# Routing, last scatter and last rows of a one-layer decoder step: logits turned, a short root, other banks and pieces

## The reference, cut to what matters

```python
mix, ... = token_mixers(rmsnorm(h, norm_mix_g), ...)
h = h + mix                                        # output projection w_out, 1024 x 1024
m = rmsnorm(h, norm_moe_g)
logits = m @ w_router + b_router                   # 1024 x 32
top_v, top_i = lax.top_k(logits, 4); gates = softmax(top_v)
h = h + sum over the four experts of gates * (act(m @ w_up[e] + b_up[e]) @ w_down[e] + b_down[e])
gate = sigmoid(rmsnorm(h, norm_ple_g) @ w_ple_gate)   # 1024 x 1024
h = h + (p @ w_ple_proj) * gate
y = rmsnorm(h, norm_final_g)
```

## Time and profile before

| | us |
|---|---|
| median of three runs (lowest, highest) | 1142.45 (1142.18, 1144.15) |
| the profiled execution's own time | 1142.76 |
| its span (first to last instruction or transfer in the trace) | 1141.0 |
| PE busy | 1088.5 (95%) |
| DVE busy | 379.8 (33%) |
| ACT busy | 156.2 (14%) |
| mean transfer rate over the span | 380 GB/s |

### The profile page before, as it was taken

The page is one execution under the profiler, slowest core; times in us unless marked ns, Lnnn a source line. Parts: engine busy times, 40 slices in busy tenths (PEclk is TensorE's granted clock), DMA queues, the critical chain, the costliest instruction groups (busy, mean ns, idle before and its releaser), DMA issues.

```text
span 1141.0 us, 16346 instructions
## 1 busy us (share of the span) xinstructions
PE 1088.5 (95%) x6463; PEld 443.6 (39%) x6463; DVE 379.8 (33%) x966; ACT 156.2 (14%) x351; POOL 32.3 (3%) x79
## 2 busy tenths in 40 slices
PE   9999999999999999999998899999999898989896
PEld 6663454333333333333333243333333333333332
DVE  3866565232222323222221223131313131313155
ACT  3543122100000000000001010000000000000022
POOL 2300120000000000000000000000000000000000
PEclk9999999999999999999999899999999999999998
DMA  8923967999999999999999999999999999999941
GB/s 300 308 111 123 380 238 294 427 427 426 428 426 427 428 428 428 428 429 428 427 430 427 428 428 426 428 427 430 427 430 428 428 429 428 428 429 427 421 156 42
DMA packets 41748, 433.86 MB, mean 380 GB/s; under 512 B 6105, under 2 KB 7265, under 8 KB 17134
## 3 DMA queue, kind: packets, MB, share of 16 engines
q1 hardware_dynamic: 40224, 428.74, 89.9%
q0 software_dynamic: 1424, 4.47, 1.2%
q10 hardware_dynamic: 62, 0.14, 0.0%
HBM read 429.03 MB, written 4.30 MB: 380 GB/s over the span
## 4 chain that ended last, share of the span: by engine, by line
PE 68%; DMA 26%; DVE 3%; ACT 1%; issue 1%; DVEq 0%; SPq 0%; ACTq 0%
PE bank L1042 28%; DMA ring<-in_w_up_dram 26%; PE bank L1088 12%; PE bank L1026 6%; PE bank L626 6%; PE bank L748 3%; PE bank L1010 3%; PE bank L650 1%; PE bank L1072 1%; PE bank L608 1%; DVE arena L1544 1%; PE bank L1117 1%; PE bank L934 1%; PE bank L1007 1%; PE bank L1078 1%; PE bank L858 1%
## 5 line engine op out<-in xcount | busy, mean ns | idle before, releaser
L1042 PE MATMUL bank<-ring,aT 128*64 128x512 f32 x1536 | 348.6, 600 | 27.6 <-DMA ring<-in_w_up_dram 27.3
L1042 PEld LDWEIGHTS bank<-ring,aT 128*64 128x64 f32 x1536 | 106.8, 137 | 253.7 <-issue 200.4
L1088 PE MATMUL bank<-ring,arena 128*64 128x512 f32 x768 | 169.6, 594 | 0.2
L1957 DVE TENSOR_TENSOR h<-h,bank 128x512 f32<-128x512 f32 (+1 forms) x96 | 65.6, 684 | 179.5 <-PE bank L1026 177.2
L1042 PE MATMUL bank<-arena,aT 128*64 128x512 f32 x512 | 115.7, 596 | 3.5 <-DMA arena<-in_w_up_dram 3.5
L1974 DVE TENSOR_SCALAR arena<-bank 128x256 f32<-128x256 f32 x64 | 27.2, 424 | 236.1 <-PE bank L1042 234.8
L1983 DVE COPY aT<-bank 64x512 f32<-64x512 f32 x32 | 22.2, 694 | 245.0 <-PE bank L1088 245.0
L1386 ACT ACTIVATE arena<-arena 128x256 f32<-128x256 f32 x64 | 26.7, 417 | 549.3 <-DVE arena L1974 549.3
L1088 PEld LDWEIGHTS bank<-ring,arena 128*64 128x64 f32 x768 | 53.8, 137 | 100.9 <-issue 98.2
L1026 PE MATMUL bank<-aT,arena 128*128 128x512 f32 (+1 forms) x192 | 83.5, 622 | 1.4 <-DVE aT L1983 0.9
L1042 PEld LDWEIGHTS bank<-arena,aT 128*64 128x64 f32 x512 | 35.2, 136 | 77.7 <-issue 69.8
(11 more groups left out here) (341 smaller groups left out, 740.5 us busy)
## 6 DMA issues: line engine op xcount, KB each, us to landing
ring<-in_w_up_dram SPq DMA_DIRECT2D x96, 2048.0 KB, 32.6
ring<-in_w_down_dram SPq DMA_DIRECT2D x48, 2048.0 KB, 33.2
arena<-in_w_up_dram SPq DMA_DIRECT2D x32, 2048.0 KB, 33.0
arena<-in_w_down_dram SPq DMA_DIRECT2D x16, 2048.0 KB, 33.3
ring<-in_w_in_dram SPq DMA_DIRECT2D x3, 2048.0 KB, 13.3
ring<-in_w_in_dram SPq DMA_DIRECT2D x4, 1024.0 KB, 11.9
ring<-in_w_out_dram SPq DMA_DIRECT2D x1, 4096.0 KB, 13.8
ring<-in_w_ple_gate_dram SPq DMA_DIRECT2D x2, 2048.0 KB, 13.5
```

The source lines that it names most:

```text
L1042: mm = pe.matmul(bank[n][CAP * hf:CAP * hf + CAP, :], xT[:, odd, 2 * j + a, :], up_cols(x, j, a, hf, n), start=False, stop=(j == 3 and a = ...
L1088: mm = pe.matmul(bank[4][CAP * hf:CAP * hf + CAP, :], actT[:, b, t, :], tile_of(x, UP_TILES + t)[:, 1024 * b + 512 * hf:1024 * b + 512 * h ...
L1957: tt(part, part, bank[5 + j % 2][at:at + ROWS[c], :], ALU.add).then_inc(s_free[j % 2], 1)
```

## The change: what it does

1. **Logits.** `turned_logits(c)` makes the router weights stationary (128 x 32) and lets the tokens move; slice k goes to rows 32(k mod 4) of a bank, so that four partial sums stand one below another. ACT copies them out (`logits_out`), and one product with `sel32` (four unit matrices of 32, one below the other) adds them up and turns them back. `sel32` is made by DVE just before `mix_done`.
2. **Root of chunk 1** (in routing, and again at the very end). ACT takes the square root; DVE takes the reciprocal and does one Newton round. A `Sqrt` without use stands ahead of it on ACT.
3. **Order in routing.** PE gathers most of chunk 0 between other work, DVE makes the selection columns right after the counts, ACT copies one turned half of chunk 1 that DVE copied before, two groups of `keep_clock` products are gone (2 and 3 products), one stays, and the last stays.
4. **Last scatter.** Each of the five products has a bank of its own (5, 6, 0, 1, 3) and waits for no addition. `moe_done` is gone; the last stage waits for each chunk by `h_ok`.
5. **Last gate product.** The second half of chunk 1 is computed as two pieces of 256 columns. ACT takes the gate halves of chunk 0 as they come. For chunk 1 DVE multiplies by the gain before the root is known; then ACT scales one half and writes it out by its own queue, DVE the other.

```diff
+            def turned_logits(c, ks=range(KD)):
...
+                    at = T_S * (k % 4)
+                    mm = pe.matmul(o[at:at + NE, 0:ROWS[c]], wrt[:, k, :], aT[:, k, TOK[c]], start=(k < 4), stop=(k >= 4))
...
+            def logits(c):
+                stored(pe, ("lgT", c))
+                o = open_bank(("lg", c))
+                close_bank(("lg", c), pe.matmul(o[0:ROWS[c], 0:NE], lgs[:, TOK[c]], sel32, start=True, stop=True))
...
+            turned_logits(2)
+            out_product(1, 0, range(4, 6))
+            pe.wait_ge(S["mix_done"], 1)
             logits(2)
-            out_product(1, 0)
+            out_product(1, 0, range(6, 8))
             turn_rows(0)
             out_product(1, 1, range(4, 6))
+            turned_logits(0)
+            turn_rows(1, (0,))
             logits(0)
-            turn_rows(1, (0,))
             out_product(1, 1, range(6, 8))
...
-            keep_clock(2, 5, parts_0)
-            logits(1)
...
+            chunk_0(range(3))
+            turned_logits(1, range(0, 4))
+            turned_logits(1, range(4, 8))
             pe.wait_ge(S["m3_ok"], 1)
-            pe.wait_ge(S["sel0_ok"], 1)
+            pe.wait_ge(S["sel0_ok"], 4)
             for d in range(KD):
                 cols, out = pass_columns(d)
...
+                pe.matmul(out, mbs[0:96, cols], sel[0:96, 0, 2, :], start=False, stop=False)
+            logits(1)
+            chunk_0(range(3, 7))
...
+            for j, ((c, hf), b) in enumerate(zip(SCATTER, LAST_BANK)):
...
+            for n, c in enumerate(ORDER):
+                pe.wait_ge(S["h_ok"], 2 * n + 2)
                 transposed(("nT", c, 0), h, c)
                 transposed(("nT", c, 1), h, c, 4)
...
             half_squares(0)
+            logits_out(0)
+            o = filled(act, ("mT", 1, 0))
+            act.activation(aT[:, 0:4, TOK[1]], o[:, :].rearrange("p (k t) -> p k t", k=4), ACT.Copy).then_inc(freed(("mT", 1, 0)), 1)
+            act.activation(rs_m[:, 0:1], ss_x[:, 1:2], ACT.Sqrt)
             half_squares(1)
+            act.wait_ge(S["hss"], 4)
+            act.wait_ge(S["pre_ok"], 1)
+            act.activation(rs_m[:, 0:1], ss_f2[:, 1:2], ACT.Sqrt, bias=ss_o[:, 1:2], scale=1.0 / D).then_inc(S["root_ok"], 1)
+            logits_out(1)
...
+            last_gate(2)
+            act.activation(rs_m[:, 2:3], ss_p[:, 1:2], ACT.Sqrt)
+            last_squares(2)
+            act.wait_ge(S["fin_ss"], 7)
+            act.wait_ge(S["pre_ok"], 2)
+            act.activation(rs_m[:, 0:1], ss_m[:, 1:2], ACT.Sqrt, bias=rs_o[:, 0:1], scale=1.0 / D).then_inc(S["root_ok"], 1)
+            act.wait_ge(S["rs_p_ok"], 3)
+            step(act.activation(yout[:, 1, 0:512], yout[:, 1, 0:512], ACT.Copy, scale=rs_f[:, 1:2]))
+            act.dma_start(O["y_prompt"].rearrange("a (c p) d -> p (a c) d", p=P)[:, 1, 0:512], yout[:, 1, 0:512])\
...
+            ts(sel_rs[:, 0, :], iota[:, :], pos[:, 0:1], mask_0, ALU.is_equal, ALU.mult).then_inc(S["sel0_ok"], 1)
+            select_2(0)
             turned_rows(1, (1,))
...
+            n_half = put(ts(half_v, ss_f2[:, 1:2], -0.5 / D, pre2, ALU.mult, ALU.add))
+            select_2(1)
+            dve.wait_ge(S["root_ok"], 1)
+            n = put(dve.reciprocal(root, rs_m[:, 0:1]))
+            select_2(2)
+            after(n)
+            n = put(stt(t, root, half_v, root, ALU.mult, ALU.mult))
+            put(dve.memset(sel[3 * T_S:, 0, 2, :], 0.0))
+            after(n)
+            stt(root, t, 1.5, root, ALU.add, ALU.mult).then_inc(S["rso_ok"], 1)
```

More of the change, by code:

```diff
@@ L422, in _ @@
             for n, c in enumerate(ORDER):
-                for hf in range(2):
+                for hf in ((1,) if c == 1 else (0, 1)):
                     half = slice(512 * hf, 512 * hf + 512)
-                    sp.wait_ge(S["yo_ok"], 2 * n + hf + 1)
+                    sp.wait_ge(S["yo_ok"], 5 if c == 1 else 2 * n + hf + 1)
                     if c < 2:
@@ L1143, in _ @@
                 else:
-                    rows_product("pg", c, w_pg)
+                    rows_product("pg", c, w_pg, halves=(0, 1) if c == 0 else (0,))
+            for n in range(2):
+                o = open_bank(("pg", 1, 1 + n))
+                for k in range(KD):
+                    mm = pe.matmul(o[:, 0:256], aT[:, k, TOK[1]], w_pg[:, k, 512 + 256 * n:768 + 256 * n],
+                                   start=(k == 0), stop=(k == KD - 1))
+                close_bank(("pg", 1, 1 + n), mm)
         @block.scalar
@@ L1367, in _ @@
             row_squares(1)
+            logits_out(2)
             part(0, 1)
@@ new lines, in row_end, with last_gate @@
+            def row_end(n, hf):
+                c = ORDER[n]
+                r = slice(0, ROWS[c])
+                half = slice(512 * hf, 512 * hf + 512)
+                act.wait_ge(S["hfin"], 2 * n + hf + 1)
+                squares(jt[r, half], h[r, c, half], (ss_f, ss_f2)[hf][r, c:c + 1], "fin_ss", 2 * n + hf)
+            gate_0(0)
+            row_end(0, 0)
+            row_end(0, 1)
+            row_end(1, 0)
+            gate_0(1)
+            row_end(1, 1)
+            def last_gate(n):
+                o = filled(act, ("pg", 1, n))
+                piece = PIECES[n]
+                act.activation(pgs[:, 1, piece], o[:, 0:piece.stop - piece.start], ACT.Sigmoid, scale=rs_p[:, 1:2])\
+                   .then_inc(freed(("pg", 1, n)), 1)
@@ L1890, in _, with select_2 @@
-            step(ts(v, ss_f2[:, 1:2], ss_o[:, 1:2], 1.0 / D, ALU.add, ALU.mult))
-            put(ts(root.bitcast(I32), v.bitcast(I32), -0.5, float(0x5f3759df), ALU.mult, ALU.add))
-            step(ts(half_v, v, -0.5, None, ALU.mult))
-            for n in range(3):
-                step(stt(t, root, half_v, root, ALU.mult, ALU.mult))
-                last = stt(root, t, 1.5, root, ALU.add, ALU.mult)
-                if n < 2:
-                    step(last)
-                else:
-                    last.then_inc(S["rso_ok"], 1)
+            def select_2(t):
+                ts(sel[T_S * t:T_S * t + T_S, 0, 2, :], iota[0:T_S, :], pos[0:T_S, NE:NE + 1], mask_2, ALU.is_equal, ALU.mult)\
+                    .then_inc(S["sel0_ok"], 1)
@@ L1921, in _ @@
             gathered(0, 1)
+            rest(1, 1)
             rest(2, 1)
@@ L1924, in _ @@
             rest(1, 2)
+            after(n_places)
             after(n)
@@ L1997, in _ @@
                     expert(q, x, x % 2 == 0)
-            add_pair(n_pass * (NE // 2) - 1)
-            for j in range(2):
-                dve.wait_ge(s_free[j], n_pass * (NE // 2 * S_READS[j]) + S_BASE)
-            dve.memset(npf[0:1, 7:8], 0.0).then_inc(S["moe_done"], 1)
+            for j, ((c, hf), b) in enumerate(zip(SCATTER, LAST_BANK)):
+                r = slice(0, ROWS[c])
+                dve.wait_ge(s_full[j % 2], n_pass * (NE // 2 * S_JOBS[j % 2]) - S_JOBS[j % 2] + j // 2 + 1 + S_BASE)
+                for f in ((hf,) if c < 2 else (0, 1)):
+                    part = h[r, c, 512 * f:512 * f + 512]
+                    at = T_S * f if c == 2 else 0
+                    tt(part, part, bank[b][at:at + ROWS[c], :], ALU.add).then_inc(S["h_ok"], 1)
             turned("nT", 7, [(c, hf) for c in ORDER for hf in range(2)])
@@ L2008, in _, with gated @@
             rstd(rs_p[:, 0:2], ss_p[:, 0:2], D, "rs_p_ok")
-            def gated(n):
+            def gated(n, halves=(0, 1)):
                 c = ORDER[n]
                 r = slice(0, ROWS[c])
-                for hf in range(2):
+                for hf in halves:
                     half = slice(512 * hf, 512 * hf + 512)
```

165 lines of the change are left out of this document (97 added, 68 removed).

## The result

The changed kernel takes 1137.03 us (median of nine executions, 1136.75 to 1140.8); nine executions of the kernel before on the same chip take 1144.15 (1142.18 to 1144.47). The ratio is 0.995, with a 95% interval of 0.9942 to 0.9959. The forecast was 1135.6 with a range of 1134.3 to 1138.0; the forecast's own range, without the rivals, ended at 1136.9. The profiled execution took 1137.14 us (span 1135.4), 5.62 less than that of before: the sum of 7.0 was 1.4 too high. Most executions of every kernel here fall into two groups some 2 us apart, because the first projection starts at 10.4 to 11.3 us in eight of the traces and at 12.4 to 13.2 in six, whatever the kernel. Six of these nine executions are in the low group and four of the nine of before, so the medians lie 7.1 us apart where the ratio stands for 5.7.

What follows compares the result with a forecast made beforehand. A weight-transfer stream at 428 GB/s bounds the middle, so time counts only before, between and after; gains of 2.4 + 2.3 + 2.3 = 7.0 us, kept as 6.8, give 1135.6 us, range 1134.3 to 1138.0 (own range 1134.4 to 1136.9).

Steps and rivals of the forecast that it cites:

- the sum of 7.0: Whole kernel: gains of 2.4 in routing, 2.3 in the last scatter and 2.3 at the end, in us.
- Part 1: Routing, before expert 0's first product at 174.96 us: expert 0 would start at 172.5, a gain of 2.4 us.
- Both paths meet at 167.2, and `choose` starts at 167.25: Routing, chunk 1: DVE's root and PE's logits both ready at 167.2 us, `choose` starting 2.2 us earlier than 169.45.
- Bounds of 0.7 to 2.8: Routing gain in us: 2.8 if both are handed over without a gap, 0.7 with slow logits, slow copy and waits.
- Rival A: Routing: blocked PE and ACT queues hold the gain back to 0.7 us, total gain 5.1, 1137.3 us; chance 0.12.
- The table load: Square root's tables on ACT in routing: load from 162.6, done with idle root at 164.1 us, hidden; 1.28 if uncovered.
- rival B: Dearer table switches in routing and end: small form, gain 5.4 us, chance 0.04; large form, gain 0, chance 0.03.
- Part 2: Last scatter, up to the gate product at 1100.83 us: it would start at 1098.5, a gain of 2.3 us.
- Part 3: The end, after the gate product: 6.6 us to the end instead of 8.92, a gain of 2.3 us.
- the same 2.47 for the write: The end: the last write was taken to last 2.47 us, as in the kernel before.
- the bound of 0.6: The end: both last writes now start together, 0.6 us for 256 KB at 428 GB/s, within the lower bound of 1.2.
- Rival C: Routing: PE's clock falls to 1.2 GHz, costing 8.5 us against 7 won, 1144 us; chance 0.03.

Runs made afterwards that it cites:

- q3: Whole change without the two filling products ahead of chunk 1's gather and without the idle root before the last squares; 1139.65 us, one execution.
- q1: Whole change with chunk 1's logits product ahead of PE's wait for the third selection, and both last halves written from SyncE's queue; 1139.35 us, one execution.
- q2: Whole change with q1's logits order, DVE's second and third selections behind the root, and a ScalarE copy between last sigmoid and idle root; 1143.75 us, one execution.
- q4: Whole change, but DVE takes chunk 2's remainder after the residual, as the kernel before does; 1139.84 us, one execution.
- p2_scatter: Kernel before with only the change's last scatter in five banks; median 1141.41 us, ratio 0.9982 to the kernel before.
- p3_end: Kernel before with only the change's last stage (gate product in pieces, short root, two write queues); median 1140.55 us, ratio 0.998 to the kernel before.
- the second round: Four kernels, q1 to q4, each the whole change with an edited routing, the first three also edited at the end; 1139.35 to 1143.75 us, one execution each.
- f4: The whole change run again unedited, beside kernels with added filling products; median 1136.98 us, ratio 0.9948 to the kernel before.

## Why the prediction was off: the mechanism held, and one meeting was placed 1.1 us too early

**What bounds it** was right: the middle is a stream that an earlier expert 0 moves whole, and the gains are in three places that add up: 1.4 + 2.2 + 1.9, with 0.4 of the anchor and −0.3 of the stream, is the 5.6 between the two spans.

**Part 1, predicted 2.4, measured 1.4: the failed step is "Both paths meet at 167.2, and `choose` starts at 167.25".** With 0.4 us added for the anchor it started at 168.37. The rest of the chain came out: from `choose` to the selection 1.80 us (1.85 in the working), from there with the idle pair to the gather 0.70 (0.5), from the gather to expert 0 2.70 (2.9). q3 shows that 0.31 of it is the idle pair. Two things account for the 1.12 us at `choose`, all but 0.07:

- 0.65 lies between DVE's copy of the turned half, done at 166.12, and `choose` at 167.97: 1.85 us where I had 1.20. Most of it is DVE's own root. It is done at 167.71, 1.59 us after the copy, where I had 1.15: the two selections take 0.31 each and not 0.25 and 0.2, and the two Newton instructions 0.58 from the last selection on and not 0.38, with a memset between them. The other 0.21 is PE's queue. I added each engine's work up by itself, took the later sum, and did not ask in which order the queue holds it: the wait for the third selection and the eight products behind it (0.39) stand ahead of the logits product, so PE idles 0.65 us with its operand ready. q1, with the other order on PE alone, gives 0.15 back, since DVE's root is next. q2, which also takes both selections out of the root, gives 0.40.
- 0.40 is the remainder of chunk 2, 1.22 us that the change puts on DVE ahead of the copies of chunk 0 (the second fence of the routing). The output projection ends at 163.88, with the anchor's 0.4 at 164.28 where I had 163.9. I gave this move no cost; q4 takes it back and gets 0.40 at `choose`.

Bounds of 0.7 to 2.8 held it. Rival A named the right kind of loss, an engine that stands in front of a blocked instruction. The 0.40 of the remainder passes through A's own place: it makes the residual, ACT's squares and ACT's copy of chunk 0 late, and PE waits 0.20 us for that copy. I had such a stall of 0.2, but for the squares alone. In q4 PE does not wait there, and the rest of the output projection starts 19.35 us after the anchor instead of 19.75. The 0.65 is at another crossing, that of chunk 1, where PE stands in front of DVE's selection.

**The table load** was hidden as said, 162.12 to 163.40. The load is 1.28, and the next activation starts 1.30 us after the load's start in the routing and 1.29 at the end (1128.88 to 1130.17). The Trainium skill's drain of 1.38 us for every switch ("ScalarE: Activation LUTs", "What ACT_TABLE_LOAD costs") is not seen in either place: the load starts 0.01 us after the end of the activation before it in the routing, and 0.02 after it at the end. Both forms of rival B fall; squares and copies ran behind the root without a load.

**Part 2, predicted 2.3, measured 2.2**: five products in 4.68 us (4.5 in the working) and transposes right behind. `p2_scatter` takes the banks and the finer waits over together, so what each of them is worth alone is not shown.

**Part 3, predicted 2.3, measured 1.9.** The last computation ended 4.13 us after the gate product, 4.1 was predicted. The mis-sized term is "the same 2.47 for the write": it took 2.9 (1132.50 to 1135.4). The two halves of 256 KB are now issued within 0.23 us of each other, and before DVE made them one behind the other. This is the bound of 0.6 that I had named and not taken. q1 shows it is not the queue; that it is the shared transfer is the reading that is left, not one that a run isolates. The load was late by under 0.1 us, not 0.6, only because DVE's multiplication started 0.48 us after the sigmoid's end. In p3_end that gap is 0.11, the load is late by 0.4 (the squares start at 1133.31, the addition before them ends at 1132.88), and the end is the same (7.0). The gap's cause stays open: it did not move with SyncE's queue (q1), a copy between (q2) or no load behind (q3).

**Rival C** did not happen in the trace of after, and does in all four traces of the second round. It had 0.03 and should have had several times that. The point that I made against it, that the largest hole is a tenth of the 3.1 us of the earlier trace rows, was no bound: PE's busy time from 166 to 170 us went from 4.00 to 3.25 of 4, in a hole of 0.65 and small ones, and the four variants whose clock fell have 3.25 to 3.38 there. But the kernel after has 3.25 as well and keeps its clock, and q3 is the same kernel up to the filling products that it leaves out at 170 us. Its price I had at 8.5 us; in q1 it is 2.9 (33.63 for the 30.69 that its order gives), since the clock falls between 168 and 169 us and is back before 176. With two of 20 at a low mean clock the median of the whole change does not feel it. What differs between an execution that falls and one that does not stays open.

## What to carry to other kernels

When two engines meet, write both queues down in order, with each small instruction at a measured length, and put the ready times on them; the sum of each engine's work is only the earliest possible meeting. Price every moved instruction by what stands behind it in its own queue, even one of 1.2 us in a stretch where its engine seems to have room. Where a change takes filling products out ahead of a short serial stretch, the holes that it opens are a risk for the clock that a single trace need not show; filling them is cheap (three products cost nothing here), though these runs do not prove that it holds the clock.

## What the runs showed of the hardware

TensorE's granted clock fell to 0.50 in the routing of four variants. PE had been busy 3.25 to 3.38 of the 4 us from 166 to 170, with no single wait over 0.7 us. It did not fall in the kernel after, at 3.25; nor did it fall there behind the wait of 3.16 us in the middle. The fall cost from 1.1 us (q3, 31.63 for 30.53) to 3.3 (q2, 33.73 for 30.44, and 1.4 more in the stream).

The two groups of times come from the clock too, not from the loads. In the six traces with the late start PE's first transposes and filling products take twice as long until some 10 us. These pieces are from the chain of f4, which starts late:

```profile
5.80 1.05 PE bank L606 x4
6.84 0.43 PE bank L590
...
10.45 0.21 PE bank L590
```

In the kernel after, which starts early, the same filling product takes 0.22 us at 7.86. Twice the time is what the lower clock cost in q1 (1.91 us for four filling products, 1.03 in after), so PE ran at 1.2 GHz up to there, although the clock column of the windows shows 1.00. Why the clock rises later in some executions stays open. The start then lies some 2 us later, and a median of five executions can fall on either side.

One GpSimd operation on 128 x 1 took 1.18 us instead of 0.27 while DVE wrote the bfloat16 remainder beside it, and 0.26 with the remainder elsewhere (q4):

```profile
157.61 1.18 POOL L556 TENSOR_SCALAR stat<-nwt,stat 128x1 f32<-128x1 f32 x1
```
